# Six throwaway weight-by-weight matrix products on TensorE taken out of each of six residual norms

## Chip, cores and metric

The kernel runs on one core of one Trainium2 chip. The metric is the device time of one execution in microseconds (us). The core has a matrix engine (TensorE, PE in the profile; its weight loads are PEld), a vector engine (VectorE, DVE), an activation engine (ScalarE, ACT), GpSimd (POOL) and a queue that issues the weight transfers (SyncE, SP). Each runs its own list of instructions in order, and they wait for each other on semaphores.

## What is computed

Two blocks of two layers each work on a residual `x` of 512 tokens by 1024 columns in float32. The first has an RG-LRU layer and a sparse-attention layer, each followed by a squared-ReLU MLP. The second, on which the change bears, is this (cut to what matters):

```python
def rms_norm(x, g, eps=1e-6):
    return x * lax.rsqrt(jnp.mean(x * x, axis=-1, keepdims=True) + eps) * g

def swiglu(x, w_gu, w_d):
    gate, up = jnp.split(x @ w_gu, 2, axis=-1)
    return (jax.nn.silu(gate) * up) @ w_d

for i in range(2):
    g = norms[i]
    x = x + 0.5 * rms_norm(swiglu(rms_norm(x, g[0]), ffn_wgu[i, 0], ffn_wd[i, 0]), g[1])
    h = rms_norm(x, g[2])
    mix = (diff_rwkv_mixer, retention_mixer)[i](h, ...)
    x = x + rms_norm(mix, g[3])
    x = x + 0.5 * rms_norm(swiglu(rms_norm(x, g[4]), ffn_wgu[i, 1], ffn_wd[i, 1]), g[5])
```

The output of each layer is normed before it is added to `x` (the "owed" norm), and the new `x` is normed again ahead of the next layer. The last norm of the first block is owed to the second block in the same way.

## The kernel before

**Tiling.** `x` stands transposed in SBUF: 8 tiles of 128 columns by 512 tokens. Float32 products are made from two halves: ScalarE rounds an operand to its high part (`whi`, `h_hi`), VectorE takes the rest (`wlo`, `h_lo`), and TensorE adds three products into one PSUM bank, high by high, high by low and low by high (lines 309, 310, 311). Weights come in chunks of 1 MB into two slots of `raw`; ScalarE and VectorE split them into the slots of `whi` and `wlo` (lines 299, 305).

**Stages.** The list `PLAN` names the stages in order: setup, norm, mixer, norm, ffn and so on. Every engine walks it with its own instructions. Six norm stages have an owed norm ahead of them: before ffn `s00`, mixer `even`, ffn `s01`, ffn `s10`, mixer `odd` and ffn `s11`. That before `s00` scales `x` itself (kind "x"); the other five scale `fsum` and add it to `x` (kind "f"), which takes VectorE one more operation for each tile. A seventh owed norm, the stage `post`, ends the kernel and is followed by the store.

**One owed norm, in order.** ScalarE squares the eight tiles (L582, and the last in two halves, L597 and L599). GpSimd adds the first six up (L682). TensorE, in `pe_owed`, multiplies a matrix of ones by this sum and by the last two squares, once for the left 256 tokens and once for the right 256, into halves of two banks (L709, L711, L716); as full float32 products they show as two records each. ScalarE takes the logarithm and the exponential of each half (L602, L603), which gives `rstd`. VectorE scales the left half, then the right, makes the new `x` and then `h_lo` of the left half (L782); ScalarE makes `h_hi` of it in between (L612). TensorE then starts the next stage in `pe_first`: six products of 256 columns on the left half of tile 0, six on the right half, then on tiles 1 to 7 with 512 columns, each of which waits for its own `h_lo` (L782 for tile 0, L741 for the others).

**The products in question.** At the end of `pe_owed`, in a norm stage only and not in `post`, TensorE waits until the first weight chunk of the next stage is split (`lo_ready`), and then makes `WARM` = 6 products of 128x128 weights by 512 columns of the same weights into bank 6 (L721). Nothing reads what they leave in the bank; the next product that uses it starts it anew. `pe_first` has its own wait for the same chunk.

Of the kernel before, what the change touches and what calls it, by code (L numbers as in the profile page):

```python
# [20 lines left out]
P = 128  # L21
S = 512
# [19 lines left out]
def build(nc, a, out):  # L42
    ctx = ExitStack()
    with ctx:
        def sb(name, shape, dt=F32):
            return ctx.enter_context(nc.sbuf_tensor(name, shape, dt))

        def sem(name):
            return ctx.enter_context(nc.semaphore(name))
# [4 lines left out]
        whi = sb("whi", [P, 2, CH], F32R)  # L54
# [17 lines left out]
        pbank = [ctx.enter_context(nc.psum_tensor(f"bank{i}", [P, S], F32)) for i in range(8)]  # L72
# [7 lines left out]
        lo_ready = sem("lo_ready")  # L80
# [106 lines left out]
        PLAN = [("setup",), ("norm", None, 0, PG["mix"]), ("rg",), ("norm", None, 0, PG["ffn"]), ("ffn", "f0")]  # L187
# [15 lines left out]
        ends = []  # L203
# [348 lines left out]

            return PLAN[stage + 1][0] == "norm" and PLAN[stage + 1][1] is None

        WARM = 6

        def owed_bank(stage, part):
            swiglu = PLAN[stage - 1][0] == "ffn" and FFN[PLAN[stage - 1][1]]["swiglu"]
            return pbank[(5 if swiglu else 3) - (part == RIGHT)][:, part]
# [144 lines left out]
        def pe_owed(pe, stage):  # L704
            j = owed_no[stage]
            pe.wait_ge(f_add, 5 * j + 5)
            for part in (LEFT, RIGHT):
                out = owed_bank(stage, part)
                pe.matmul(out, ones[:, :], acc[:, part], start=True, stop=False)  # L709
                pe.wait_ge(f_sq, KT * j + 7)  # L710
                pe.matmul(out, ones[:, :], tmp[:, 4, part], start=False, stop=False)  # L711
                if part == LEFT:
                    pe.wait_ge(f_sqa, j + 1)
                else:
                    pe.wait_ge(f_sq, KT * j + 8)
                pe.matmul(out, ones[:, :], tmp[:, 5, part], start=False, stop=True).then_inc(f_sum, 1)  # L716
            if PLAN[stage][0] == "norm":
                n = ends[stage - 1]
                pe.wait_ge(lo_ready, n + 1)
                for r in range(WARM):  # L720
                    pe.matmul(pbank[6][:, :], whi[:, n % 2, 0:P], whi[:, n % 2, 0:S], start=True, stop=True)  # L721

        def pe_sum(pe, stage):
            j = norm_no[stage - 1]
# [2480 lines left out]
        @block.tensor  # L3205
        def _(pe):
            for stage, step in enumerate(PLAN):
                enter(pe, stage)
                if step[0] == "setup":
                    pe_setup(pe)  # L3210
                elif step[0] in ("norm", "post") and step[1] is not None:
                    pe_owed(pe, stage)
                elif step[0] == "ffn":
                    pe_ffn(pe, step[1], stage)
                elif step[0] == "rg":
                    pe_rg(pe, stage)
                elif step[0] == "nsa":
                    pe_nsa(pe, stage)
                elif step[0] == "even":
                    pe_even(pe, stage)  # L3220
                elif step[0] == "odd":
                    pe_odd(pe, stage)
                elif step[0] == "store":
                    pe_store(pe, stage)
                leave(pe, "pe")
# [25 lines left out]
```

## Time and profile before

| | us |
|---|---|
| median of 3 runs | 3592.9 |
| lowest and highest of them | 3591.96, 3597.85 |
| the profiled execution | 3590.76 |
| its span, first to last instruction | 3588.8 |
| TensorE busy in it | 3487.4 (97%) |
| VectorE busy | 1945.9 (54%) |
| ScalarE busy | 1247.5 (35%) |
| GpSimd busy | 444.4 (12%) |
| mean granted TensorE clock, share of full | 0.992 |

The span leaves 1.96 us of the execution's time outside it. Durations and starts below are of this one execution, which is 2.1 us shorter than the median. A row of the timeline gives the start from the beginning of the span, then how long an instruction or a merged run of them took, and in square brackets how long the engine had been idle before it and what ended that. Consecutive products overlap, so that the distance between two starts, not the duration, is the pace.

### The profile page before, as it was taken

The page shows a single profiled execution, that of the slowest core. Times are in us where ns is not written, and L with a number is a line of the kernel's source. Part 1 is how long each engine was busy: PE and PEld are TensorE (multiplying, and loading weights), DVE is VectorE, ACT ScalarE, POOL GpSimd, SP SyncE. Part 2 cuts the span into 40 slices and gives each one's busy share as a digit, 9 for nine tenths or more (in the row PEclk, how much of TensorE's full clock was granted, in tenths as well). Part 3 has the DMA queues.
Part 4 walks back from the last instruction along what each step waited for, and adds up shares of the span by engine and source line. Part 5 has one row for each costly group of instructions (what it writes and reads, how often), then busy time and mean ns, then how long its engine had stood idle before and what let it go on. Part 6 is the DMA issues. An engine that isn't in the chain of part 4 may idle for free.

```text
span 3588.8 us, 47528 instructions
## 1 busy us (share of the span) xinstructions
PE 3487.4 (97%) x18803; PEld 2784.9 (78%) x18803; DVE 1945.9 (54%) x2698; ACT 1247.5 (35%) x1776; POOL 444.4 (12%) x358
## 2 busy tenths in 40 slices
PE   8999999999999999999998999999999999999998
PEld 6888888545888878887777788878888787778887
DVE  5655563465555555445567554556445534465555
ACT  5532232464422242223644332233222422242222
POOL 1220011010100021112023010111111000011111
PEclk9999999999999999999999999999999999999999
DMA  3332234200222323232100132222232222213231
GB/s 119 106 109 94 94 94 94 47 1 13 94 94 94 104 85 100 88 105 88 59 25 15 53 109 97 94 82 96 92 105 94 82 82 82 82 59 106 94 101 64
DMA packets 232545, 295.80 MB, mean 82 GB/s; under 512 B 21893, under 2 KB 201464, under 8 KB 232392
## 3 DMA queue, kind: packets, MB, share of 16 engines
q1 hardware_dynamic: 230864, 290.48, 25.4%
q0 software_dynamic: 1152, 3.05, 0.4%
q8 instruction: 109, 1.79, 0.2%
q14 instruction: 44, 0.36, 0.0%
q10 hardware_dynamic: 376, 0.12, 0.0%
HBM read 291.53 MB, written 2.10 MB: 82 GB/s over the span
## 4 chain that ended last, share of the span: by engine, by line
PE 88%; DVE 5%; ACT 3%; issue 2%; POOL 1%; DMA 0%; POOLq 0%; SPq 0%; DVEq 0%; ACTq 0%
PE bank L309 25%; PE bank L311 25%; PE bank L310 25%; POOL tmp L682 1%; PE bank L338 1%; PE bank L339 1%; PE bank L340 1%; PE bank L2969 1%; ACT whi L299 1%; DVE wlo L305 1%; PE bank L1490 1%; PE bank L2436 1%; PE bank L1575 1%; PE bank L1559 1%; ACT fsum L1649 0%
## 5 line engine op out<-in xcount | busy, mean ns | idle before, releaser
L309 PE MATMUL bank<-h_hi,whi 128*128 128x512 f32 x2780 | 1094.9, 394 | 22.8 <-DVE h_lo L741 9.4
L311 PE MATMUL bank<-h_hi,wlo 128*128 128x512 f32 x2780 | 1081.1, 389 | 0.0
L310 PE MATMUL bank<-h_lo,whi 128*128 128x512 f32 x2780 | 1080.8, 389 | 0.0
L299 ACT ACTIVATE whi<-raw 128x2048 fp32r<-128x2048 f32 x266 | 508.6, 1912 | 1249.3 <-PE bank L311 1196.7
L305 DVE TENSOR_TENSOR wlo<-raw,whi 128x2048 fp32r<-128x2048 f32 x266 | 613.3, 2306 | 321.8 <-ACT whi L299 321.8
L309 PEld LDWEIGHTS bank<-h_hi,whi 128*128 128x128 f32 x2780 | 522.7, 188 | 149.8 <-issue 29.9
L311 PEld LDWEIGHTS bank<-h_hi,wlo 128*128 128x128 f32 x2780 | 522.6, 188 | 108.9
L310 PEld LDWEIGHTS bank<-h_lo,whi 128*128 128x128 f32 x2780 | 522.9, 188 | 108.3 <-issue 3.6
L309 PE MATMUL bank<-u_hi,whi 128*128 128x512 f32 x1408 | 548.9, 390 | 4.7 <-DVE arena L3045 2.4
L310 PE MATMUL bank<-u_lo,whi 128*128 128x512 f32 x1408 | 547.8, 389 | 0.0
L311 PE MATMUL bank<-u_hi,wlo 128*128 128x512 f32 x1408 | 547.8, 389 | 0.0
L457 POOL TENSOR_TENSOR tmp<-tmp,rstd 128x512 f32<-128x512 f32 x88 | 175.5, 2015 | 1112.6 <-ACT tmp L426 1112.3
L309 PEld LDWEIGHTS bank<-u_hi,whi 128*128 128x128 f32 x1408 | 264.3, 188 | 62.1 <-issue 3.7
L310 PEld LDWEIGHTS bank<-u_lo,whi 128*128 128x128 f32 x1408 | 264.3, 188 | 54.9 <-issue 0.2
L311 PEld LDWEIGHTS bank<-u_hi,wlo 128*128 128x128 f32 x1408 | 264.3, 188 | 54.9
L516 DVE TENSOR_TENSOR fsum<-fsum,bank 128x512 f32<-128x512 f32 x316 | 211.5, 685 | 82.0 <-PE bank L311 81.8
L516 DVE TENSOR_TENSOR x<-x,bank 128x512 f32<-128x512 f32 x255 | 168.9, 684 | 50.3 <-PE bank L311 50.2
L490 DVE TENSOR_TENSOR tmp<-bank,tmp 128x512 f32<-128x512 f32 x88 | 60.9, 692 | 247.9 <-PE bank L311 219.8
L475 DVE TENSOR_TENSOR tmp<-bank,rstd 128x512 f32<-128x512 f32 x88 | 60.1, 691 | 229.3 <-PE bank L311 214.6
L434 ACT ACTIVATE u_hi<-tmp 128x512 fp32r<-128x512 f32 x88 | 55.7, 633 | 329.0 <-DVE tmp L490 329.0
L479 DVE SCALAR_TENSOR_TENSOR tmp<-bank,rstd 128x512 f32<-128x512 f32 x64 | 44.1, 692 | 180.4 <-PE bank L311 180.4
L438 ACT ACTIVATE tmp<-tmp 128x512 f32<-128x512 f32 x64 | 40.4, 632 | 256.6 <-DVE tmp L479 256.6
(438 smaller groups left out, 3100.8 us busy)
## 6 DMA issues: line engine op xcount, KB each, us to landing
raw<-in_ffn_wgu SPq DMA_DIRECT2D x88, 1024.0 KB, 5.1
raw<-in_ffn_wd SPq DMA_DIRECT2D x44, 1024.0 KB, 5.1
raw<-in_mlp_w_up SPq DMA_DIRECT2D x32, 1024.0 KB, 5.5
raw<-in_mlp_w_down SPq DMA_DIRECT2D x32, 1024.0 KB, 5.0
raw<-in_odd_w_in SPq DMA_DIRECT2D x24, 1024.0 KB, 5.2
raw<-in_even_w_in SPq DMA_DIRECT2D x13, 1024.0 KB, 5.3
raw<-in_rg_w_in SPq DMA_DIRECT2D x8, 1024.0 KB, 5.5
raw<-in_odd_w_out SPq DMA_DIRECT2D x8, 1024.0 KB, 5.1
```

The lines of the kernel that those rows point to most:

```text
L299: e.activation(whi[:, n % 2, :], raw[:, n % 2, :], ACT.Copy).then_inc(hi_ready, 1)
L305: e.tensor_tensor(wlo[:, n % 2, :], raw[:, n % 2, :], whi[:, n % 2, :].bitcast(F32), ALU.subtract).then_inc(lo_ready, 1)
L309: pe.matmul(o, w_hi, r_hi, start=first, stop=False)
L310: pe.matmul(o, w_hi, r_lo, start=False, stop=False)
L311: return pe.matmul(o, w_lo, r_hi, start=False, stop=last)
L434: e.activation(u_hi[:, u, :], tmp[:, 2 + j, :], ACT.Copy).then_inc(uhi_done, 1)
L438: e.activation(tmp[:, 2 + j, :], tmp[:, j, :], ACT.Square)
L457: e.tensor_tensor(tmp[:, j, :], tmp[:, j, :], rstd[:, :], ALU.mult).then_inc(scaled, 1)
L475: ins = e.tensor_tensor(tmp[:, j, :], pbank[half + j][:, :], rstd[:, :], ALU.mult)
L479: ins = e.scalar_tensor_tensor(tmp[:, j, :], pbank[half + j][:, :], 0.0, rstd[:, :], ALU.max, ALU.mult)
L490: e.tensor_tensor(tmp[:, 2 + j, :], pbank[half + 2 + j][:, :], tmp[:, j, :], ALU.mult)\
L516: e.tensor_tensor(dst[:, m, :], dst[:, m, :], src[:, :], ALU.add).then_inc(added, 1)
```

## The change

`pe_owed` ends after the products with ones. The six products of L721, the wait for `lo_ready` ahead of them and the constant `WARM` go; nothing is put in their place. Over the kernel that is 36 products and 36 weight loads in six norm stages.

```diff
@@ -551,8 +551,6 @@
         def early_lo(stage):
 
             return PLAN[stage + 1][0] == "norm" and PLAN[stage + 1][1] is None
-
-        WARM = 6
 
         def owed_bank(stage, part):
@@ -714,11 +712,6 @@
                 else:
                     pe.wait_ge(f_sq, KT * j + 8)
                 pe.matmul(out, ones[:, :], tmp[:, 5, part], start=False, stop=True).then_inc(f_sum, 1)
-            if PLAN[stage][0] == "norm":
-                n = ends[stage - 1]
-                pe.wait_ge(lo_ready, n + 1)
-                for r in range(WARM):
-                    pe.matmul(pbank[6][:, :], whi[:, n % 2, 0:P], whi[:, n % 2, 0:S], start=True, stop=True)
```

## Rows read from the trace of the kernel before

**Rows 1.** The page: the span, its busy time, the chain that ended last.

```profile
span 3588.8 us, 47528 instructions
PE 3487.4 (97%) x18803; PEld 2784.9 (78%) x18803; DVE 1945.9 (54%) x2698; ACT 1247.5 (35%) x1776; POOL 444.4 (12%) x358
...
PE 88%; DVE 5%; ACT 3%; issue 2%; POOL 1%; DMA 0%; POOLq 0%; SPq 0%; DVEq 0%; ACTq 0%
```

**Rows 2.** Groups by line and form: busy us, mean ns of one | idle before.

```profile
L721 PE MATMUL bank<-whi 128*128 128x512 f32 x36 | 11.4, 455 | 0.0
```

**Rows 3.** Timeline around the norm before s00, all engines: start, us, engine, line.

```profile
1267.93 0.70 PE L709 MATMUL bank<-tmp,ones 128*128 128x256 f32 x2 [2.45 <-POOL tmp L682]
...
1270.44 1.74 PE L721 MATMUL bank<-whi 128*128 128x512 f32 x6
...
1270.83 0.47 ACT L602 ACTIVATE rstd<-bank,eps 128x256 f32<-128x256 f32 x1 [0.37 <-PE bank L716]
...
1272.19 0.48 DVE L782 SCALAR_TENSOR_TENSOR h_lo<-x,par,h_hi 128x256 fp32r<-128x256 f32 x1
...
1272.82 0.35 PE L309 MATMUL bank<-h_hi,whi 128*128 128x256 f32 x1 [0.63 <-DVE h_lo L782]
...
1274.60 0.36 PE L309 MATMUL bank<-h_hi,whi 128*128 128x256 f32 x1 [0.83 <-DVE h_lo L782]
```

**Rows 4.** Stretches of the span: us; busy by engine, then PEclk, the granted clock.

```profile
1266.65:1270.06 3.41, 2.13 (x10) 1.90 (x11) 0.00 (x0) 1.07 (x4) 1.23 (x1) 1.00 0.00 0
...
1638.70:1642.11 3.41, 3.41 (x10) 2.69 (x9) 0.91 (x2) 1.15 (x3) 0.00 (x0) 0.50 0.00 0
...
2044.89:2048.30 3.41, 3.41 (x13) 2.82 (x12) 3.15 (x6) 2.37 (x4) 0.00 (x0) 0.50 0.00 0
2048.30:2051.71 3.41, 3.41 (x17) 2.78 (x15) 3.41 (x6) 1.89 (x4) 0.00 (x0) 1.00 0.01 2
...
2410.11:2413.53 3.42, 3.42 (x10) 2.70 (x9) 0.91 (x2) 1.52 (x4) 0.00 (x0) 0.50 0.00 0
...
3574.06:3577.47 3.41, 2.37 (x10) 1.43 (x8) 3.31 (x6) 0.00 (x0) 0.00 (x0) 0.50 0.00 0
```

**Rows 5.** Timeline of TensorE alone, where it waited: five owed norms and the store.

```profile
1637.48 0.70 PE L709 MATMUL bank<-tmp,ones 128*128 128x256 f32 x2 [2.73 <-POOL tmp L682]
...
1643.84 0.36 PE L309 MATMUL bank<-h_hi,whi 128*128 128x256 f32 x1 [0.45 <-DVE h_lo L782]
...
2042.55 0.35 PE L309 MATMUL bank<-h_hi,whi 128*128 128x256 f32 x1 [0.64 <-DVE h_lo L782]
...
2044.54 0.35 PE L309 MATMUL bank<-h_hi,whi 128*128 128x256 f32 x1 [1.04 <-DVE h_lo L782]
...
2408.69 0.70 PE L709 MATMUL bank<-tmp,ones 128*128 128x256 f32 x2 [2.39 <-POOL tmp L682]
...
2414.86 0.36 PE L309 MATMUL bank<-h_hi,whi 128*128 128x256 f32 x1 [0.27 <-DVE h_lo L782]
...
2416.86 0.36 PE L309 MATMUL bank<-h_hi,whi 128*128 128x256 f32 x1 [1.05 <-DVE h_lo L782]
...
2780.21 0.70 PE L709 MATMUL bank<-tmp,ones 128*128 128x256 f32 x2 [2.38 <-POOL tmp L682]
...
2791.29 0.50 PE L309 MATMUL bank<-h_hi,whi 128*128 128x512 f32 x1 [0.47 <-DVE h_lo L741]
...
3573.54 0.67 PE L963 MATMUL bank<-ident,x 128*128 128x128 f32 x4 [2.53 <-DVE x L757]
```

**Rows 6.** Timeline of TensorE alone: the pace at half clock, then at full.

```profile
2045.67 0.63 PE L309 MATMUL bank<-h_hi,whi 128*128 128x512 f32 x1
...
2048.23 0.43 PE L309 MATMUL bank<-h_hi,whi 128*128 128x512 f32 x1
...
2787.87 0.40 PE L309 MATMUL bank<-h_hi,whi 128*128 128x512 f32 x1
...
2790.43 0.39 PE L311 MATMUL bank<-h_hi,wlo 128*128 128x512 f32 x1
```

## The prediction, made before the result was known

> **What bounds the kernel now.** I read the page first. TensorE is busy 3487.4 of 3588.8 us, and 88% of the chain that ended last is TensorE's [rows 1]. Work taken off TensorE shortens the kernel only where TensorE was late, so the next view is the groups by line. The 36 products in question take 11.4 us together and have no idle time ahead of them [rows 2]. That number is not yet a gain: it must be seen who was waiting behind them.
>
> The timeline of all engines around one norm answers that [rows 3]. TensorE starts the products with ones at 1267.93, after 2.45 us of idleness, and the six products at 1270.44, which end at 1270.44 + 1.74 = 1272.18. The first product of the next stage starts at 1272.82, and the row says that TensorE was idle for 0.63 us and that the `h_lo` of L782 ended this. The path to that `h_lo` is ScalarE's logarithm at 1270.83, which waited for the last product with ones, then the exponential, then VectorE up to 1272.19 and its 0.48 us. None of it reads bank 6. After six short products TensorE is idle again for 0.83 us, for the right half of the same tile. So in a norm the path runs through ScalarE and VectorE, and the six products lie beside it. The other norms look the same: the waits for L782 are 0.64 and 1.04 us in the norm before s01, and 0.45 and 0.27 us are left of the first one in the norms before `even` and s10 [rows 5].
>
> The last view is the granted clock by stretch [rows 4]. It is at one of two levels, 1.00 (2.4 GHz) or 0.50 (1.2 GHz). Around the owed norms it fell three times, each time for 3.41 us: at 1638.70 and 2410.11, after TensorE had been idle for 2.73 and 2.39 us ahead of the products with ones, and at 2044.89, after it had been idle 0.64 and 1.04 us around six short products [rows 4, 5]. After an idleness of 2.45 us it did not fall [rows 3, 4]. The same sort of pause therefore costs the clock in one place and not in another; where in time it falls decides. The profile's execution had its luck with this, and another one will have other luck.
>
> **The change part by part.**
>
> *The products themselves.* 36 products of 396 ns at the pace of about 0.23 us are 36 x 0.23 = 8.3 us of TensorE's time. All of it lies in front of a wait for `h_lo` that still had 0.27 to 0.64 us left when they were done [rows 3, 5]. Taking them away makes this wait longer and nothing earlier: 0 us.
>
> *The wait for `lo_ready`.* The chunk had been split before the norm, and the next stage waits for it anyway: 0 us. No queue but TensorE's is touched, no DMA moves, and what is queued behind the products on TensorE is only the product that waits for `h_lo`.
>
> *The idle time that they covered.* This is the part with a price. Without them TensorE is idle from about 1270.8, where L602 sees the ones done, to 1272.82, works for 0.9 us, and is idle for 0.83 us (s00) or 1.04 us (the others) more [rows 3, 5]. That is 2.0 + 0.8 or 1.0 = some 3.0 us of idleness with 0.9 us of work in it, more than the pause at 2042.55 to 2044.54 (0.64 + 1.04 us), after which the clock fell, and in sum no less than the pauses of 2.39 and 2.73 us after which it fell. The nearest row without such products is the end of the kernel: there the ones are followed by 2.53 us of idleness, and the clock was at 0.50 from 3574.06 [rows 4, 5]. I take it that the clock falls in all six norms. The bounds are none more than now and all six.
>
> *The price of one low stretch.* At half clock seven starts from 2045.67 to 2048.23 stand 2.56 / 6 = 0.427 us apart; at full clock twelve starts from 2787.87 to 2790.43 stand 2.56 / 11 = 0.233 us apart [rows 6]. A stretch of 3.41 us full of products loses 3.41 x (1 - 0.233 / 0.427) = 1.55 us. What of it reaches the end can be read from whole ffn stages, from the right half of tile 0 to the next idleness. In s01, with the stretch at 2044.89: 2408.69 - 2.39 - 2044.54 = 361.76 us. In s10, without one: 2780.21 - 2.38 - 2416.86 = 360.97 us. The low stretch cost 0.79 us [rows 5]. Stage s00, whose VectorE has one operation less for each tile, took 1637.48 - 2.73 - 1274.60 = 360.15 us [rows 3, 5], 0.82 us less than s10. That 0.82 us is the cover: VectorE makes the tiles of kind "f" more slowly than TensorE first uses them (0.47 us of it is the wait for L741 at 2791.29), and 1.55 - 0.82 = 0.73 us agrees with the 0.79 us measured. So a stretch that lies wholly behind the right half costs 0.79 us in a norm of kind "f" and 1.55 us before s00, where the cover is not there.
>
> *How much of the stretch lies there.* It may begin anywhere from the left half's start to a little after the right half's. In the earliest case about 1.4 us of 3.41 lie behind the right half's start (the left half's six products are slower too, but a wait of 0.83 to 1.05 us takes that up). It loses 1.4 x 0.454 = 0.64 us: all of it before s00, nothing under the cover elsewhere. The latest case is that of s01. The middle is 1.1 us before s00 and 0.4 us in a norm of kind "f".
>
> *The sum.* 1.1 + 4 x 0.4 us for five norms that had no such stretch, and 0.4 - 0.79 = -0.4 us for s01, which had the dearest: 1.1 + 1.6 - 0.4 = +2.3 us. The bounds of the unknown count and place: 0, and 1.55 + 4 x 0.79 = +4.7 us. Against the profiled execution that is 3590.76 + 2.3 = 3593.1 us; the median of the runs shown is 2.1 us above that execution, and 3592.9 + 2.3 = **3595.2 us** is what I predict. The span would grow by as much, and the 1.96 us around it stay.
>
> *A rule beside it.* The cost read from the trace is 0.79 us for a low stretch of 3.41 us, because VectorE's pace hides the rest. The Trainium skill (TensorE: Matmul & The Clock Gate, section "Terms") prices throttled time by its share of lost clock, half of the time at half clock. By that rule six stretches less the one that is there already would be 5 x 1.7 = 8.5 us and the time an estimated 3601.4 us. No number above rests on it. The same page (section "What's actually happening") says that the slow phase varies from run to run of one kernel; the trace agrees in that idleness of 2.39 us was followed by a fall and 2.45 us was not.
>
> **The rivals.**
>
> *A: the clock stays low twice as long, and the kernel is slower.* After a fall the clock has to come back. At 1638.70, 2044.89 and 2410.11 it came back after 3.41 us in which TensorE was busy without a pause; at the store it stayed at half while TensorE was busy 2.37 of 3.41 us [rows 4]. A stretch that begins at the left half has a pause in it, and may be followed by a second one. Two are 6.83 us. They lose 6.83 x 0.454 = 3.1 us if they begin at the right half, and 4.8 x 0.454 = 2.2 us if at the left, in the middle 2.65 us, less the cover of 0.82 us elsewhere than in s00: 1.8 us. The sum is 2.65 + 4 x 1.8 + (1.8 - 0.79) = +10.9 us, 3603.8 us. It decides from four norms on, since the bound of slower, 0.2%, is 7.2 us. Against it: the products of the store are of another kind (transposes), so its row is a weak witness. The rule of the skill above, which leaves the cover out, comes near to the same time.
>
> *B: the clock falls no more often than now.* 3592.9 us. For it: idleness of 2.45 us ahead of the ones left the clock at 1.00, and the new one is of 2.0 us with work behind it. Against it: that work is short and the second pause follows. The Trainium skill (same page, section "Why this matters for your kernels") warns only of idle gaps longer than any single one here, which is on this rival's side.
>
> *C: the six products were in the way.* Where the clock is low when they begin, they need 6 x 0.427 = 2.56 us at a distance of 2.4 us from the ones to `h_lo`, and the first real product could start up to 0.4 us late. Before s10 the wait left was 0.27 us, so it did not happen in this execution [rows 5]. In five norms it would be at most 5 x 0.4 = 2.0 us: 3590.9 us. It can be faster by more than 0.2% only if something else shifts with it.
>
> **How the numbers follow.** The forecast has 0.5, A 0.2, B 0.2, C 0.1. A measurement of this kernel can tell about 0.2% from no change, 7.2 us: the three runs before are 5.9 us apart, which the two low stretches ahead of the ones explain, since they come by chance. They make the way from L709 to the first real product 1643.84 - 1637.48 = 6.36 us and 2414.86 - 2408.69 = 6.17 us where it is 4.89 us without one [rows 3, 5], 1.3 to 1.5 us each. The forecast, B and C lie inside the bound but for 0.02 of C; of A about 0.15 lies beyond it, and 0.01 goes each way for what I don't see. That gives slower 0.16, faster 0.03, same 0.81. The range goes from C with some of the chance of the runs, 3591.2, to the middle of A, 3603: less than 0.1 is left out at either end.
>
> **What the profile after would show.** The group L721 gone, and the waits of `h_lo` L782 in 12 rows longer by about 8 us together. The starts of L309 at the same 4.89 us behind L709 wherever the clock is full. Stretches at 0.50 that begin between the left half of tile 0 and the first tiles, in five or six of the six norms. The stage s00 longer than 360.15 us by 0.6 to 1.6 us, and the stages s01, s10 and s11 between 361.0 and 361.8 us. I am wrong if the clock is still at 1.00 there (B), if stretches of over 3.41 us stand there and the ffn stages take over 362.3 us (A), or if the first real product comes sooner than 4.89 us after L709 (C).

## The result and the profile after

| | before | after |
|---|---|---|
| median, us (10 runs each) | 3595.78 | 3604.17 |
| lowest and highest | 3590.74, 3609.11 | 3602.62, 3613.52 |
| the profiled execution | 3590.76 | 3607.08 |
| its span | 3588.8 | 3605.2 |
| its mean granted TensorE clock | 0.992 | 0.985 |

The medians are 8.4 us apart. The ratio of the runs is 1.0029 with a 95% interval of 1.0019 to 1.0039: by it the kernel became slower by 10.4 us (7 to 14), a little more than the 0.2% that I had called the limit of what can be told. The prediction was 3595.2 us in a range of 3591.2 to 3603.0. Both are missed, by 9.0 and 1.2 us.

The page after, in its first lines:

```profile
span 3605.2 us, 47456 instructions
...
PE 3494.5 (97%) x18767; PEld 2790.5 (77%) x18767; DVE 1945.6 (54%) x2698; ACT 1247.7 (35%) x1776; POOL 446.7 (12%) x358
```

TensorE has 36 products fewer than in [rows 1] and is busy 7.1 us longer: among the products that are left, some have become slower. The two kernels' rows for the first products of a stage, from the groups by line and form (busy us, mean ns of one | idle before), of after:

```profile
L309 PE MATMUL bank<-h_hi,whi 128*128 128x256 f32 x24 | 9.9, 412 | 17.0 <-DVE h_lo L775 17.0
```

and of before:

```profile
L309 PE MATMUL bank<-h_hi,whi 128*128 128x256 f32 x24 | 7.8, 324 | 9.4 <-DVE h_lo L782 9.4
```

L775 is L782 of before (and L707 is L709, L734 is L741). The idle time went up by 7.6 us, and the mean product by 88 ns. In the timeline of TensorE after, the rows that answer to [rows 3, 5] are:

```profile
1268.60 0.70 PE L707 MATMUL bank<-tmp,ones 128*128 128x256 f32 x2 [2.45 <-POOL tmp L680]
...
1273.48 0.35 PE L309 MATMUL bank<-h_hi,whi 128*128 128x256 f32 x1 [2.02 <-DVE h_lo L775]
...
1275.26 0.55 PE L309 MATMUL bank<-h_hi,whi 128*128 128x256 f32 x1 [0.83 <-DVE h_lo L775]
...
1641.03 0.70 PE L707 MATMUL bank<-tmp,ones 128*128 128x256 f32 x2 [2.74 <-POOL tmp L680]
...
1645.91 0.36 PE L309 MATMUL bank<-h_hi,whi 128*128 128x256 f32 x1 [2.02 <-DVE h_lo L775]
...
1647.91 0.55 PE L309 MATMUL bank<-h_hi,whi 128*128 128x256 f32 x1 [0.89 <-DVE h_lo L775]
...
2047.66 0.70 PE L707 MATMUL bank<-tmp,ones 128*128 128x256 f32 x2 [0.41 <-POOL tmp L680]
...
2054.54 0.55 PE L309 MATMUL bank<-h_hi,whi 128*128 128x256 f32 x1 [0.54 <-DVE h_lo L775]
...
2419.41 0.70 PE L707 MATMUL bank<-tmp,ones 128*128 128x256 f32 x2 [2.40 <-POOL tmp L680]
...
2424.29 0.36 PE L309 MATMUL bank<-h_hi,whi 128*128 128x256 f32 x1 [2.02 <-DVE h_lo L775]
2426.29 0.55 PE L309 MATMUL bank<-h_hi,whi 128*128 128x256 f32 x1 [0.77 <-DVE h_lo L775]
...
2791.39 0.70 PE L707 MATMUL bank<-tmp,ones 128*128 128x256 f32 x2 [2.40 <-POOL tmp L680]
```

The wait for the left half has grown from 0.63 to 2.02 us, and the product that ends it comes 1273.48 - 1268.60 = 4.88 us after the ones, as in [rows 3]. It is 4.88 us in five of the six norms; in that before s11 a stretch at half clock lies on the products with ones, and it is 6.57 us, no less than the 6.17 and 6.36 us that such norms took with the six products. So the six products had delayed nothing. The loss comes behind it. The stretches of the span at half clock (us; busy by engine, then PEclk, the granted clock), one row for the time before the first fall and one for the time behind it:

```profile
1271.07:1274.48 3.41, 1.34 (x8) 0.77 (x6) 2.48 (x5) 2.78 (x7) 0.00 (x0) 1.00 0.00 0
1274.48:1277.89 3.41, 2.63 (x9) 2.44 (x10) 3.41 (x7) 3.13 (x6) 0.00 (x0) 0.50 0.02 5
1277.89:1281.31 3.42, 3.42 (x9) 2.64 (x8) 3.42 (x6) 3.15 (x6) 0.00 (x0) 0.50 0.00 0
1281.31:1284.72 3.41, 3.41 (x16) 2.78 (x15) 2.96 (x5) 3.06 (x7) 0.00 (x0) 1.00 0.00 0
1646.54:1653.36 6.82, 5.93 (x19) 4.79 (x18) 6.56 (x12) 4.31 (x9) 0.00 (x0) 0.50 0.01 2
...
2052.72:2059.55 6.83, 6.29 (x21) 5.25 (x21) 6.57 (x12) 4.26 (x8) 0.00 (x0) 0.50 0.01 4
2424.77:2431.60 6.83, 6.06 (x20) 4.93 (x20) 6.58 (x12) 4.31 (x8) 0.00 (x0) 0.50 0.01 2
2796.83:2803.65 6.82, 5.99 (x20) 4.85 (x19) 6.56 (x12) 4.31 (x8) 0.00 (x0) 0.50 0.01 2
...
3220.08:3226.91 6.83, 5.85 (x18) 4.75 (x17) 6.57 (x12) 4.31 (x8) 0.00 (x0) 0.50 0.01 2
...
1950.32:1957.15 6.83, 6.16 (x47) 4.73 (x48) 1.69 (x6) 1.49 (x4) 0.00 (x0) 0.50 0.00 0
1991.28:2001.52 10.24, 8.17 (x79) 5.80 (x67) 3.93 (x14) 4.34 (x10) 0.00 (x0) 0.50 0.01 2
```

The last two of these rows lie deep in the mixer `even`; the others lie behind the six norms. In all six norms the clock falls to half 0.2 to 1.0 us after the left half has begun, and stays there for 6.83 us, twice as long as the only stretch of this sort before, at 2044.89 [rows 4].

The ffn stages, from the right half of tile 0 to the next idleness, by the prediction's own reckoning: s00 took 1641.03 - 2.74 - 1275.26 = 363.03 us (before 360.15, so +2.88 us), s01 2419.41 - 2.40 - 2054.54 = 362.47 us (361.76 before with one stretch, 360.97 in s10 without: +1.50 against none), s10 2791.39 - 2.40 - 2426.29 = 362.70 us (+1.73).

The span grew by 16.4 us, more than the timed difference. The two profiled executions are not typical ones: that of before is 5.0 us below the median of its kernel (3595.78 - 3590.76), that of after 2.9 us above (3607.08 - 3604.17), and without these 7.9 us the 16.3 us between the two executions are the 8.4 us between the medians. The largest single piece is in a place that the change doesn't touch: from its right half to the next idleness, the mixer `even` took 2047.66 - 0.41 - 1647.91 = 399.34 us, where before it was 2037.66 - 0.40 - 1645.84 = 391.42 us by the trace of before. Some 1.7 of these 7.9 us belong behind the norm. The rest goes with stretches at half clock deep in the mixer: 1950.32 and 1991.28 above, and one of 3.42 us at 1909.36, 20.5 us together. Before it had two of 3.41 us there:

```profile
1863.98:1867.39 3.41, 3.41 (x27) 2.51 (x26) 1.14 (x4) 1.19 (x2) 0.00 (x0) 0.50 0.02 5
1976.62:1980.03 3.41, 3.41 (x49) 3.41 (x46) 0.84 (x2) 0.40 (x1) 0.00 (x0) 0.50 0.77 239
```

Whether these are chance was the first question to the chip.

### The profile page after: what moved, and what is told of

It is laid out like the page before. It is cut to its first block, busy times and chain, and to the rows that moved or that the text cites. A ratio compares the mean times of both kernels' runs of the same rounds, so it can differ in the third digit from the quotient of the medians.

```text
span 3605.2 us, 47456 instructions
## 1 busy us (share of the span) xinstructions
PE 3494.5 (97%) x18767; PEld 2790.5 (77%) x18767; DVE 1945.6 (54%) x2698; ACT 1247.7 (35%) x1776; POOL 446.7 (12%) x358
## 4 chain that ended last, share of the span: by engine, by line
PE 89%; DVE 5%; ACT 3%; issue 2%; POOL 1%; DMA 0%; POOLq 0%; SPq 0%; DVEq 0%; ACTq 0%
PE bank L309 25%; PE bank L311 25%; PE bank L310 25%; POOL tmp L680 1%; PE bank L338 1%; PE bank L340 1%; PE bank L339 1%; PE bank L2962 1%; ACT whi L299 1%; DVE wlo L305 1%; PE bank L2429 1%; PE bank L1568 1%; PE bank L1483 1%; PE bank L1552 1%; ACT fsum L1642 1%
```

## The experiments

The theory (T) by now is that the whole loss is the half clock behind the norms; it is twice what I had forecast because a low stretch that has TensorE's second pause in it does not end after 3.41 us. It has three rivals: the difference is mostly chance in `even` (U); what counts is that TensorE has instructions, not how much work they are (V); the length of a stretch has nothing to do with a pause in it (W). The kernels ran in two groups, four and three, each group with 29 or 30 runs of before beside it (medians 3596.3 and 3596.4 us).

**The changed kernel again.** No edit.

> The changed kernel once more, for a second trace with another timing of the low stretches and a comparison on this chip. Theory T (the price is low clock right behind each norm, twice as long as I had forecast because TensorE pauses in it): low stretches of 6.83 us at the start of at least five of the six next stages, s00 about 363.0 us and s10 about 362.7 us from the right half of tile 0 to the next idleness, and some 8 to 10 us more than before in the timed rounds. Theory U (chance: most of the 16.4 us between the two spans is the 7.9 us by which the mixer even was longer, which has nothing to do with the norms): even falls back to within 2 us of 391.4 us, and the timed difference to before is under 4 us.

Measured: 3605.0 us median, ratio 1.0025 (1.0016 to 1.0034), 8.8 us over before. The mixer `even` took 394.10 us in its trace, 5.2 us less than in the first, and the timed difference to before stayed. U falls: what `even` adds is chance of the single execution, the timed 8 to 10 us are not. (The span of this trace is 3605.1 us all the same. What comes ahead of s00 took 4.2 us more than in the first trace, and three stretches lie on products with ones where that had one.) The low stretches are 6.83 us long in four of six norms here. In the other two, before s00 and s01, they are 3.41 us. One of each sort:

```profile
2052.74:2056.15 3.41, 3.04 (x10) 2.77 (x11) 3.29 (x6) 1.65 (x3) 0.00 (x0) 0.50 0.02 5
2424.79:2431.62 6.83, 5.98 (x17) 5.05 (x18) 6.58 (x12) 4.31 (x8) 0.00 (x0) 0.50 0.01 2
```

The first began at 2052.74, late in the second pause, whose end was at 2053.11, so that only 0.37 us of it lay inside; of the 1.05 us pause that ended at 2425.64, 0.85 us lay in the second. The short stretch cost stage s01 0.6 us, against 1.5 us in the first trace. The other short one, before s00, had 0.34 us of pause in it, and s00 took 361.0 us, not the 363.0 that I had expected; s10 took 362.9 us, near the 362.7. My "at least five of six" was too much; that the pause decides the length fits.

**Six small products.**

```diff
-                    pe.matmul(pbank[6][:, :], whi[:, n % 2, 0:P], whi[:, n % 2, 0:S], start=True, stop=True)
+                    pe.matmul(pbank[6][:, 0:64], whi[:, n % 2, 0:P], whi[:, n % 2, 0:64], start=True, stop=True)
```

> The kernel before, with the six products of each norm cut from 512 columns to 64: as many instructions, waits and weight loads, but the first pause is filled with only a little matrix work. Theory T (what counts is how much TensorE works in the pause): low stretches as in the changed kernel, time within 3 us of it, some 7 to 10 us over before. Rival V (what counts is that TensorE has instructions to run, or that the program is as long as before): as before, within 3 us.

Measured: 3603.6 us, ratio 1.0020 (1.0008 to 1.0031). As many products and weight loads as before, the same wait for `lo_ready` ahead of them, and most of the loss is there (7.4 us by the medians). In its timeline and stretches, around the norm ahead of `odd`:

```profile
2791.07 0.94 PE L721 MATMUL bank<-whi 128*128 128x64 f32 x6
...
2793.44 0.36 PE L309 MATMUL bank<-h_hi,whi 128*128 128x256 f32 x1 [1.43 <-DVE h_lo L782]
...
2795.44 0.55 PE L309 MATMUL bank<-h_hi,whi 128*128 128x256 f32 x1 [0.78 <-DVE h_lo L782]
...
2793.93:2800.76 6.83, 6.05 (x20) 4.92 (x20) 6.57 (x12) 4.31 (x8) 0.00 (x0) 0.50 0.00 0
```

The idle time is 1.43 us, shorter than after the change, and the clock falls all the same: for 6.83 us in four of the six norms, for 3.41 us before s00 (with 0.51 us of the second pause in the stretch), and not at all before s01. V falls.

**The second pause filled, the first left empty.** The changed kernel, with this in `pe_first`:

```diff
             part(0, 0, LEFT)
+            for r in range(3):
+                pe.matmul(pbank[6][:, :], whi[:, n % 2, 0:P], whi[:, n % 2, 0:S], start=True, stop=True)
             part(0, 0, RIGHT)
```

> The changed kernel, with three products of 128x512 between the left and the right half of tile 0, where TensorE waits 0.83 to 1.04 us; the first pause of 2.02 us stays empty. Theory T: the clock still falls behind the first pause in more than half of the norms, but there is no pause in the low stretch any more, so it lasts 3.41 us and not 6.83 us and costs up to 0.8 us (1.6 us before s00): in all 3 to 5 us over before, half of what the change cost. Rival W (the length of a low stretch has nothing to do with a pause in it): stretches of 6.83 us still, 8 to 10 us over before.

Measured: 3597.6 us, ratio 1.0007 (0.9997 to 1.0017): 1.4 us over before by the medians, and not to be told from it. The interval, 1 us below to 6 us above before, rules out the 8 to 10 us of W, but not the 3 to 5 us that I had expected. This is the run that separates T from W. Its timeline and stretches at two norms:

```profile
1273.97 0.36 PE L309 MATMUL bank<-h_hi,whi 128*128 128x256 f32 x1 [2.02 <-DVE h_lo L775]
...
1275.15:1278.56 3.41, 3.41 (x13) 2.58 (x12) 3.41 (x7) 3.32 (x6) 0.00 (x0) 0.50 0.03 5
...
1639.94 0.84 PE L707 MATMUL bank<-tmp,ones 128*128 128x256 f32 x2 [2.72 <-POOL tmp L680]
...
2418.03 0.35 PE L309 MATMUL bank<-h_hi,whi 128*128 128x256 f32 x1 [2.02 <-DVE h_lo L775]
...
2418.62:2422.03 3.41, 3.41 (x15) 2.95 (x14) 3.28 (x7) 1.91 (x4) 0.00 (x0) 0.50 0.02 5
2422.03:2425.44 3.41, 3.41 (x17) 2.80 (x16) 3.28 (x6) 2.40 (x5) 0.00 (x0) 1.00 0.00 0
...
2783.55 0.97 PE L707 MATMUL bank<-tmp,ones 128*128 128x256 f32 x2 [2.39 <-POOL tmp L680]
```

The first pause is 2.02 us as after the change, and the clock still falls, in five of six norms (not before s01) and nearly as early, 0.5 to 1.2 us after the left half has begun. But all five stretches last 3.41 us. W falls. Such a short stretch costs next to nothing in a norm of kind "f": from the left half to the next idleness, s10 took 2783.55 - 2.39 - 2418.03 = 363.13 us, where before, without a stretch, it took 2780.21 - 2.38 - 2414.86 = 362.97 us [rows 5]; after the change it was 2791.39 - 2.40 - 2424.29 = 364.70 us. By the same measure the short stretch cost 0.2 us in `odd` and 0.1 us in s11. Before s00 it cost more: 1639.94 - 2.72 - 1273.97 = 363.25 us, against 1637.48 - 2.73 - 1272.82 = 361.93 us before, +1.3 us. I had expected half of the loss to stay; these come to less than 2 us in the stages where I can read it.

**All pauses filled.** The kernel before with its six, the three of the last experiment, and eight more in `pe_owed` ahead of the ones, in the five norms in which TensorE waits there (`fb` is the PSUM bank that they write; the edit of the last experiment is left out here):

```diff
             j = owed_no[stage]
+            if PLAN[stage][0] == "norm" and PLAN[stage - 1][0] != "even":
+                n = ends[stage - 1]
+                pe.wait_ge(lo_ready, n + 1)
+                fb = {"f1": 0, None: 6}.get(PLAN[stage - 1][1] if PLAN[stage - 1][0] == "ffn" else None, 6)
+                for r in range(8):
+                    pe.matmul(pbank[fb][:, :], whi[:, n % 2, 0:P], whi[:, n % 2, 0:S], start=True, stop=True)
             pe.wait_ge(f_add, 5 * j + 5)
```

> The kernel before with more of the same products: its six, three more between the left and the right half of tile 0, and eight ahead of the products with ones in the five norms in which TensorE waits 2.4 to 2.75 us for GpSimd's sum. Theory T: no low stretch is left around the norms, in which before had three that cost 1.48, 1.29 and 0.79 us in its profile: 3 to 4 us faster than before on the average, 0.1%. Rival X (the added products stand in the way of the real ones, since they are in front of them on the same queue): slower than before by up to 0.3 us for each of eleven pauses, 3 us.

Measured: 3589.6 us, ratio 0.9978 (0.9968 to 0.9989), 6.7 us faster than before by the medians and 4 to 12 us by the interval. It beats both kernels, and its 8 runs are close together (3585.2 to 3590.6 us, the 30 of before 3588.8 to 3608.6). TensorE's timeline around the norm ahead of s10, and then two stretches of 20 us, around the norms ahead of `even` and of s10, the last three columns of which begin with the granted clock:

```profile
2407.27 2.12 PE L711 MATMUL bank<-whi 128*128 128x512 f32 x8
2409.60 0.70 PE L715 MATMUL bank<-tmp,ones 128*128 128x256 f32 x2 [0.21 <-POOL tmp L682]
...
2414.48 0.36 PE L309 MATMUL bank<-h_hi,whi 128*128 128x256 f32 x1 [0.65 <-DVE h_lo L788]
2415.27 0.85 PE L886 MATMUL bank<-whi 128*128 128x512 f32 x3
...
2416.48 0.36 PE L309 MATMUL bank<-h_hi,whi 128*128 128x256 f32 x1 [0.36 <-DVE h_lo L788]
...
1634.00:1654.00 20.00, 17.88 (x80) 13.54 (x79) 12.82 (x23) 11.13 (x21) 5.79 (x5) 1.00 0.11 38
...
2403.00:2423.00 20.00, 18.20 (x82) 13.83 (x81) 13.02 (x23) 11.15 (x22) 5.97 (x5) 1.00 0.11 37
```

Short pauses are left, of 0.21, 0.65 and 0.36 us; no real product comes later (2414.48 - 2409.60 = 4.88 us), so X falls. The granted clock is 1.00 around all six norms. The gain was larger than the 3 to 4 us that I had reckoned from the one trace of before.

**Two parts of it alone.** Before and the three of the second pause:

> The kernel before with its six products, and three more between the left and the right half of tile 0; nothing ahead of the products with ones. Theory T: the six keep the clock up behind the first pause and the three close the second, so no low stretch begins between the left half and the first tiles, where before has one in its trace (at 2044.89, 0.79 us) ; those ahead of the ones (1.3 to 1.5 us each, by chance) stay. 0 to 1.5 us faster than before. Rival X (more products in front of the real ones cost time): up to 0.3 us more in each norm.

Measured: 3596.7 us, ratio 1.0003 (0.9993 to 1.0014). No change can be told: no low stretch lies behind the ones in its trace, as expected, but what that is worth is too little to be seen. Two stretches lie on the ones, where the way to the left half is 6.49 and 6.58 us. Before and the eight ahead of the ones:

> The kernel before with its six products, and eight more ahead of the products with ones in the five norms in which TensorE waits 2.4 to 2.75 us there. Theory T: no low stretch falls on the products with ones any more, so that the way from their first to the left half is 4.88 us in all six norms; this is most of the gain of the kernel with all three fillings, 2 to 6 us faster than before. Rival Y (that gain was chance on that chip or came from the second pause): within 2 us of before.

Measured: 3591.0 us, ratio 0.9984 (0.9975 to 0.9993), 5.4 us faster. The way from the ones to the left half is 4.88 or 4.89 us in all six norms. One low stretch of 3.41 us stands behind a norm, as in before. Y falls, and most of the gain of the kernel with all pauses filled, 5.4 of 6.7 us by the medians, is from here: in the traces of the kernels without this filling, stretches on the ones, 1.3 to 1.7 us each, lie in one to five of the five norms.

**Half the products.** `WARM = 3` for 6.

> The kernel before with three products of 512 columns in each norm for six: the first pause is then some 1.3 us. Theory T: the clock falls in some norms, where the two pauses come to lie together, and a stretch that has the second pause in it lasts 6.83 us: between before and the changed kernel, 2 to 6 us over before. If what counts were only that some full products run there, as before.

Measured: 3593.4 us, ratio 0.9990 (0.9979 to 1.0002). This is a miss: I expected 2 to 6 us over before, and it can't be told from before. Its trace is of one of its longer executions, 3603.3 us; all five norms in which TensorE waits for GpSimd's sum have a stretch on the ones in it, 1.6 to 1.7 us each. Low stretches lie behind three norms, and two of those are short:

```profile
1648.23:1651.64 3.41, 2.84 (x10) 2.58 (x11) 3.28 (x7) 1.45 (x3) 0.00 (x0) 0.50 0.00 0
2051.00:2054.41 3.41, 3.17 (x11) 2.82 (x12) 3.28 (x6) 1.78 (x3) 0.00 (x0) 0.50 0.00 0
2795.11:2801.93 6.82, 6.13 (x18) 5.09 (x19) 6.56 (x12) 4.25 (x7) 0.00 (x0) 0.50 0.01 2
```

They begin 1.3 to 1.8 us after the left half has begun and not 0.2 to 1.0 us as after the change. The short ones have 0.57 and 0.24 us of the second pause in them, the long one 0.69 us, and in the other three norms the clock does not fall behind the ones. Why the kernel is not slower is so argued from one trace, not shown. By the times, three products of 512 columns do what six do, as far as can be told, while six of 64 columns do little.

## Why the prediction was wrong

*What bounds the norm* was right. The products covered nothing but idle time, the first wait grew by 1.4 us or more in each norm, and wherever the clock was full on the ones the first real product came 4.88 us after them as before. The twelve waits grew by 7.6 us together, where I had said about 8. The products' own 8.3 us of TensorE's time were worth 0 us. Rival C falls with it: nothing had been in the way.

*The clock falls in all six norms* was right: six of six in the trace after, against one before, 0.2 to 1.0 us after the left half had begun, inside the stretch of time that I had given. Rival B is out: no single pause around the norms was longer than 2.75 us, and the clock fell all the same.

*The price of one low stretch* is the step that failed. The prediction took the length of 3.41 us from the three stretches of [rows 4] and let the new ones have it too. In those three TensorE had been busy without a pause; the new ones have 0.5 to 1.0 us of the pause between the halves in them and last 6.83 us. With that pause filled they lasted 3.41 us again. So a stretch put at 0.4 us in a norm of kind "f" and at 1.1 us before s00 cost 1.5 to 2.0 us and 2.9 us. Rival A says this in so many words, and I gave it 0.2, with the row of the store's transposes as the only one in its favour. That was not the only one. The trace of before has two stretches of twice 3.41 us elsewhere, one at its start, one in the first block's sparse-attention mixer:

```profile
13.95:17.37 3.42, 0.00 (x0) 0.00 (x0) 3.11 (x3) 3.31 (x6) 0.00 (x0) 0.50 0.08 26
17.37:20.78 3.41, 3.33 (x8) 2.68 (x9) 2.17 (x3) 3.38 (x5) 0.00 (x0) 0.50 0.90 277
...
686.38:689.79 3.41, 3.39 (x13) 1.35 (x10) 1.78 (x12) 2.45 (x9) 0.00 (x0) 0.50 0.48 125
689.79:693.21 3.42, 3.42 (x13) 2.01 (x14) 1.55 (x3) 0.60 (x1) 0.00 (x0) 0.50 0.92 182
```

So the length of 3.41 us was never a fixed one. The forecast's side had no row with a pause in it: no stretch in the trace of before had one and ended after 3.41 us. A should have had at least as much as the forecast.

*A's own working* was near. It had 1.8 us for a norm of kind "f" and 2.65 us before s00; the trace has 1.50 us (s01), 1.73 us (s10) and 2.88 us. Five such norms and s00 make about 5 x 1.7 + 2.9 = 11.4 us, less the 0.79 us that s01 had already: 10.6 us, against 10.4 us by the ratio, 8.4 us by the medians and A's 10.9 us. That the sum comes so near is in part luck: it takes all six stretches at 6.83 us, and in the repeat four of six were (where they cost up to 2.0 us, in s10). For `odd` and s11 I have the same sort of figure, 1.7 us each; for `even` it can't be separated from the mixer's own stretches, and stands at 1.7 us as an estimate from its neighbours.

*The cover of 0.82 us* held, and did at least what I had let it. Of a single stretch 0.16 us was left in s10 when it began 0.6 us behind the left half's start (363.13 against 362.97 us with the second pause filled), and 1.3 us before s00, where I had said that the cover is missing. The forecast's middles of 0.4 and 1.1 us were of the right size for single stretches, and the bound of 4.7 us would have held had the stretches been single: the kernel in which they were is 1.4 us over before by the medians, 2.5 us by the ratio.

*The rule beside it.* The Trainium skill's price of throttled time (TensorE: Matmul & The Clock Gate, section "Terms") gave an estimate of 3601.4 us, nearer than mine. It was near for two faults that cancel. The estimate took half the length of the stretches and all of their lost clock. For the real stretches of 6.83 us the same price would be 3.4 us each, 18.8 us in all once the one that was there is taken off; the stages show 1.5 to 1.7 us for four of them and 2.9 us for s00 (the sixth can't be read). The trace is against it wherever another engine sets the pace in a part of the low time.

*The range* ended at 3603.0 us, called the middle of A, but A's own figure is 3603.8 us. It left out more than half of a case of 0.2, and not "less than 0.1" at that end. The interval was drawn around the median of the three runs shown, 3592.9 us; ten runs of before put it at 3595.8 us, and 2.9 of the 9.0 us that the forecast is off are that. I had named the chance stretches on the ones as the cause of the spread, and had then taken the median as if three runs could settle it. The two in the trace come to 1.48 + 1.29 = 2.8 us, so that they did not account for the 5.9 us between those runs either. How much is left to chance shows in the two traces of the changed kernel: one stretch on the ones in the first, three in the second.

## What to carry to other kernels

Where TensorE waits on a short path of other engines, ask of every pause not only how long it is but what follows. Here a fall of the granted clock behind one pause cost 0.1 to 0.2 us where VectorE set the pace (1.3 us where it didn't) if TensorE was then kept busy, and 1.5 to 2.0 us (2.9 us) if a second pause lay in the low stretch. Throwaway products in such pauses were worth their place in this kernel, also in a pause in which the trace at hand happens to show no fall, since that changes from run to run: without the six it was 8 to 10 us slower, and with eight more ahead of the ones it was 5.4 us faster than with the six alone. When a step of a prediction rests on a duration, look whether the rows that it is from share the property that the new case lacks.

## What the runs showed of the hardware

- Around these norms the granted clock came back after 3.41 us in all five stretches with the second pause filled. After the change it came back after 6.83 us in six of six, with 0.54 to 0.98 us of the pause in the stretch. In the repeat four stretches were long (0.57 to 1.01 us of pause in them) and two short (0.34, 0.37 us); with 64 columns four were long (0.60 to 1.00 us) and one short (0.51 us); with three products one was long (0.69 us) and two short (0.24, 0.57 us). So 0.57 us was seen with either length.
- Busy time alone does not say when the clock comes back: in the first block's sparse-attention mixer of before, whose products are other and mostly smaller ones, it stayed at half for 6.83 us from 686.38 with TensorE busy for 6.81 us of them. Why is open.
- Six products of 64 columns left most of the loss in place (ratio 1.0020 to before, 1.0029 and 1.0025 without any); with three of 512 columns no difference to six can be told (0.9990, 0.9979 to 1.0002).
- The time of one and the same kernel moves with the time at half clock. Worked out from the span and mean granted clock of each of the 59 runs of before beside the experiments, the correlation is 0.94, and a us at half clock goes with some 0.3 us of span. The changed kernel's 21 runs have 30 us more at half clock than these on the average, 99 against 68 us, which at that rate is 9 us, an estimate of the size of the timed loss.
